# Layer norms over the partition axis: a provisional mean while the residual is made, elementwise sums of squares, a later correction of the variance

## The reference

```python
def layer_norm(x, g, b):                 # layers 0 and 1, after each residual
    mu = x.mean(-1, keepdims=True)
    var = jnp.square(x - mu).mean(-1, keepdims=True)
    return (x - mu) * lax.rsqrt(var + LN_EPS) * g + b
def rms_norm(x, g):                      # layers 2 and 3, ahead of mixer and FFN
    return x * lax.rsqrt(jnp.mean(x * x, axis=-1, keepdims=True) + EPS) * g
h = layer_norm(DN_ALPHA * h + g1 * mixer(u), ln1_g[l], ln1_b[l])
u = h * (1.0 + sc2) + sh2                # what the FFN reads
h = layer_norm(DN_ALPHA * h + g2 * swiglu(u), ln2_g[l], ln2_b[l])
```

## Time and profile before

| | us |
|---|---|
| median of 3 runs | 4056.42 (4052.18 to 4057.0) |
| the profiled execution, its own time | 4060.49 |
| its span on the engines | 4058.7 |
| PE busy | 3738.0 (92%) |
| DVE, ACT, POOL busy | 1667.6, 1322.4, 1464.4 |
| mean granted TensorE clock | 0.951 of full speed |

### The profile page before, as it was taken

The page is one execution under the profiler, slowest core; times in us unless marked ns, Lnnn a source line. Parts: engine busy times, 40 slices in busy tenths (PEclk is TensorE's granted clock), DMA queues, the critical chain, the costliest instruction groups (busy, mean ns, idle before and its releaser), DMA issues. The chain is left out here.

```text
span 4058.7 us, 38874 instructions
## 1 busy us (share of the span) xinstructions
PE 3738.0 (92%) x15948; PEld 2878.6 (71%) x15948; DVE 1667.6 (41%) x2218; ACT 1322.4 (33%) x2140; POOL 1464.4 (36%) x779
## 2 busy tenths in 40 slices
PE   4999888898999999988899899989898999899999
PEld 3887655676888688755577688857467887577887
DVE  5223554436343322455443634344545212374220
ACT  2334234322322234423432232225432222333221
POOL 1232232343455322222234345434124544204543
PEclk9998898999999999989899999999899999899999
DMA  5233211244554323421124355433015333202332
GB/s 176 83 104 104 57 42 35 72 133 120 160 167 134 114 78 94 117 55 42 37 70 132 109 169 168 135 89 90 16 37 148 96 96 91 60 13 87 94 95 77
DMA packets 566895, 385.25 MB, mean 95 GB/s; under 512 B 13518, under 2 KB 504222, under 8 KB 566718
## 3 DMA queue, kind: packets, MB, share of 16 engines
q1 hardware_dynamic: 564494, 379.56, 32.1%
q10 hardware_dynamic: 2224, 3.21, 0.3%
HBM read 379.25 MB, written 2.10 MB: 94 GB/s over the span
## 5 line engine op out<-in xcount | busy, mean ns | idle before, releaser
L144 POOL TENSOR_TENSOR wlo<-raw,whi 128x1024 fp32r<-128x1024 f32 (+2 forms) x538 | 1280.7, 2390 | 2068.2 <-ACT whi L140 2067.8
L174 PE MATMUL ps<-UH,whi 128*128 128x512 f32 x2656 | 1069.7, 403 | 57.8 <-ACT UH L140 36.8
L174 PE MATMUL ps<-UH,wlo 128*128 128x512 f32 x2656 | 1050.4, 395 | 11.3 <-POOL wlo L144 11.2
L174 PE MATMUL ps<-UL,whi 128*128 128x512 f32 x2656 | 1050.2, 395 | 5.1 <-DVE UL L144 3.9
L140 ACT ACTIVATE whi<-raw 128x1024 fp32r<-128x1024 f32 (+2 forms) x538 | 545.8, 1025 | 545.7 <-PE ps L174 253.5
L174 PEld LDWEIGHTS ps<-UH,whi 128*128 128x128 f32 x2656 | 507.6, 191 | 185.2 <-ACT UH L140 43.0
L174 PEld LDWEIGHTS ps<-UH,wlo 128*128 128x128 f32 x2656 | 507.9, 191 | 126.6 <-POOL wlo L144 18.0
L174 PEld LDWEIGHTS ps<-UL,whi 128*128 128x128 f32 x2656 | 506.6, 191 | 123.7 <-DVE UL L144 12.9
L152 DVE SCALAR_TENSOR_TENSOR ACC<-raw,SM,ACC 128x512 f32<-128x512 f32 x336 | 379.6, 1130 | 25.0 <-DMA raw<-in_w_ada 2.8
L174 PE MATMUL ps<-GH,whi 128*128 128x512 f32 x704 | 274.8, 390 | 0.0
L174 PE MATMUL ps<-GL,whi 128*128 128x512 f32 x704 | 274.0, 389 | 0.0
(11 more groups left out here) (295 smaller groups left out, 4442.9 us busy)
## 6 DMA issues: line engine op xcount, KB each, us to landing
raw<-in_w_in SPq DMA_DIRECT2D x170, 512.0 KB, 3.9
raw<-in_w SPq DMA_DIRECT2D x120, 512.0 KB, 5.2
raw<-in_w_ada SPq DMA_DIRECT2D x96, 512.0 KB, 4.9
raw<-in_ada_w SPq DMA_DIRECT2D x96, 512.0 KB, 4.5
raw<-in_ffn_w_gate SPq DMA_DIRECT2D x44, 512.0 KB, 3.9
raw<-in_ffn_w_up SPq DMA_DIRECT2D x44, 512.0 KB, 3.8
raw<-in_ffn_w_down SPq DMA_DIRECT2D x32, 512.0 KB, 3.8
raw<-in_ev_w_in SPq DMA_DIRECT2D x20, 512.0 KB, 4.0
```

Source lines behind the costliest of these rows:

```text
L144: return self.e.tensor_tensor(o, a, b, op).then_inc(*self.done(*keys))
L174: m = self.e.matmul(o, l, r, start=start, stop=stop)
```

## The change

In the layer norms:

- After residual tile 4 PE sums `CSUM` (tiles 0 to 3) into a provisional mean. DVE subtracts it (`less`) from tiles 5, 6, 7 ahead of their residual step and from 0 to 4 behind it, one instruction a tile.
- ACT squares the tiles as they come (`SQ_AT`, `SQ_ORDER`), POOL adds the squares into `P2`.
- Behind the last tile PE does four matmuls with ones: of `CSUM` (now tiles 4, 5, 6) and `H` 7 for the rest of the mean, of `P2` and the last square for the sum of squares. ACT copies the rest of the mean to `MU` and squares it, DVE corrects the variance, and DVE (tiles 0 to 3) and POOL (4 to 7) subtract `MU`.
- Scale columns `SG` and `KG` are worked out ahead. The scaled `H` for the next residual is made later (`dve_scaled`, in the first two steps of the FFN or at the start of attention).

In all norms from n1 on: `nrm` is one instruction `H*SG*R`; ACT adds the shift as it makes `UH`, and DVE as it makes `UL`. POOL's tiles are now 3, 5, 7, with a second DVE instruction for the shift. The RMS columns are made ahead of the last residual tile.

```diff
     def lo_lane(nid, kt):
-        return "pool" if nid != "n0" and kt in (1, 3, 5) else "dve"
+        return "pool" if nid != "n0" and kt in (3, 5, 7) else "dve"
+    def dve_u(v, nid, shift, centred):
+        sq, _, _, R, _ = norm_tiles(nid)
+        for kt in range(NT + 1):
+            if kt < NT:
+                s = sq[kt % 2][:, :]
+                if kt > 1:
+                    v.wait_ge(*on("act", "uh", nid, kt - 2))
+                    v.wait_ge(*on(lo_lane(nid, kt - 2), "ul", nid, kt - 2))
...
+                v.stt(s, H[:, kt, :], SG[:, kt:kt + 1], R[:, :], ALU.mult, ALU.mult, None if pool else ("s", nid, kt))
+                if pool:
+                    v.wait_ge(*v.prior())
+                    v.ts(s, s, shift[:, kt:kt + 1], None, ALU.add, None, ("s", nid, kt))
+            if kt and lo_lane(nid, kt - 1) == "dve":
...
+                v.stt(UL[:, kt - 1, :], sq[(kt - 1) % 2][:, :], shift[:, kt - 1:kt], UH[:, kt - 1, :].bitcast(F32),
+                      ALU.add, ALU.subtract, ("ul", nid, kt - 1))
+    SQ_ORDER = (0, 1, 5, 2, 3, 6, 4, 7)
+    SQ_AT = {5: (0, 1, 2), 6: (3, 4, 5), 7: (6, 7)}
+    def pe_norm_ln(p, nid, rid, mod):
...
+        p.wait_ge(*on("dve", "cs", nid))
+        p.mm(od[:, :], ones, CSUM[:, :], True, False)
+        p.wait_ge(*on("pool", "p2", nid, 6))
+        p.mm(ov[:, :], ones, P2[:, :], True, False)
+        p.wait_ge(*on("dve", "H", rid, 7))
+        p.mm(od[:, :], ones, H[:, 7, :], False, True, ("dsum", nid))
+        p.wait_ge(*on("act", "sq", nid, 7))
+        p.mm(ov[:, :], ones, sq_tile(nid, 7)[:, :], False, True, ("var", nid))
+    def dve_norm_ln(v, nid, rid, g, b, mod):
...
+        v.wait_ge(*on("act", "dc", nid))
+        centre(0)
+        centre(1)
...
+        v.stt(R[:, :], ps(("var", nid))[:, :], 1.0 / D, P2[:, :], ALU.mult, ALU.subtract, ("var", nid))
+        centre(2)
+        centre(3)
+        v.wait_ge(*on("act", "sd", nid))
+        v.recip(R[:, :], R[:, :])
+    def pool_norm_ln(g, nid):
+        MU = norm_tiles(nid)[4]
+        g.wait_ge(*on("act", "dc", nid))
+        for kt in range(4, NT):
+            g.wait_ge(*on("act", "sq", nid, SQ_ORDER.index(kt)))
+            g.tt(H[:, kt, :], H[:, kt, :], MU[:, :], ALU.subtract, ("Hd", nid, kt))
     def dve_residual(...):
+                elif m == 4:
+                    v.wait_ge(*on("pe", "prov", nid))
+                    for x in (5, 6, 7):
+                        v.wait_ge(*kept(x))
+                        less(x, ("pre", nid, x))
...
+                    less(0, ("Hp", nid, 0))
+                    less(1, ("Hp", nid, 1))
     def act_residual(a, rid, nid, sums, chunks_to):
...
             act_split(a, chunks_to(m))
+                for j in SQ_AT.get(m, ()):
+                    a.wait_ge(*less_mean(nid, rid, SQ_ORDER[j]))
+                    if j > 2:
+                        a.wait_ge(*on("pool", "p2", nid, j - 2))
+                    a.af(sq_tile(nid, j)[:, :], H[:, SQ_ORDER[j], :], ACT.Square, ("sq", nid, j))
+    def pool_residual(g, rid, nid, sums):
+        for m in range(NT):
+            pool_split(g, soon(rid, m))
+            for j in SQ_AT.get(m, ()) if sums == "means" else ():
+                if 0 < j < 7:
+                    g.wait_ge(*on("act", "sq", nid, j))
...
+                    g.tt(norm_tiles(nid)[1][:, :], norm_tiles(nid)[1][:, :], sq_tile(nid, j)[:, :], ALU.add, ("p2", nid, j))
     def dve_ffn(v, f, nid=None):
             dve_fill(v)
+            if nid and m < 2:
+                for kt in range(4 * m, 4 * m + 4):
+                    dve_scaled(v, nid, kt)
```

More of the change, by code:

```diff
@@ L593, in dve_decay @@
         v.ts(C8, C8, 8.0, None, ALU.mult, None, "c8")
+    tiles = {}
     def norm_tiles(nid):
[L598 to L602, removed]
+        if nid not in tiles:
+            tiles[nid] = (ring("nrm", 88, 2, 512), at("nsq", 94, [128, S], F32, BASE), at("nsum", 96, [128, S], F32, BASE),
+                          at("nrd", 92, [128, S]), at("nmu", 98, [128, S], F32, BASE))
+        return tiles[nid]
@@ L616, in pool_lo @@
     def pool_lo(g, nid):
         sq = norm_tiles(nid)[0]
[L618 to L624, removed]
-        for kt in range(NT):
-            p.wait_ge(*on("act", "sqr", nid, kt))
-            p.mm(o[:, :], ones, sq[kt % 2][:, :], kt == 0, kt == NT - 1, ("tot", nid, kt))
-        if not mod:
-            o = bank(p, AUX, ("sums", nid), ("act", ("sd", "n5")))
-            for kt in range(NT):
-                p.wait_ge(*on("act", "sqn", nid, kt))
-                p.mm(o[:, :], ones, sq[kt % 2][:, :], kt == 0, kt == NT - 1, ("ton", nid, kt))
@@ L634, in dve_norm_ln @@
[L634 to L638, removed]
-            blk, jsc, jsh = mod
-            wait_ada(v, blk, jsc, jsh)
-            v.ts(S1, ad(blk, jsc), 1.0, None, ALU.add, None)
-            v.wait_ge(*v.prior())
[L643 to L650, removed]
-        v.wait_ge(*on("act", "sd", nid))
-        v.recip(R[:, :], R[:, :])
-        v.wait_ge(*v.prior())
[L654 to L691, removed]
@@ new lines, in sq_tile @@
+    def sq_tile(nid, j):
+        sq, P2, _, _, _ = norm_tiles(nid)
+        return sq[(j - 1) % 2] if j else P2
+    def pe_norm_ln(p, nid, rid, mod):
+        sq, P2, CSUM, _, _ = norm_tiles(nid)
+        od = bank(p, AUX, ("dsum", nid), ("act", ("dc", nid)))
+        ov = bank(p, AUX, ("var", nid), ("dve", ("var", nid)))
+        p.wait_ge(*on("dve", "cs", nid))
[6 more added lines that the diff above has]
+        p.mm(ov[:, :], ones, sq_tile(nid, 7)[:, :], False, True, ("var", nid))
+        if not mod:
+            o = bank(p, AUX, ("sums", nid), ("act", ("sd", "n5")))
+            for kt in range(NT):
+                p.wait_ge(*on("act", "sqn", nid, kt))
+                p.mm(o[:, :], ones, sq[kt % 2][:, :], kt == 0, kt == NT - 1, ("ton", nid, kt))
@@ L731, in act_norm_rms, with pe_residual @@
         a.af(R[:, :], ps(b)[:, :], ACT.Sqrt, ("sd", nid), scale=1.0 / D, bias=EPS_RMS)
[L732 to L743, removed]
+        act_u(a, nid, ad(mod[0], mod[2]))
+    def pe_residual(p, rid, nid, name, lay, KT, XH, XL, xw, sums, fill=False):
         for m in range(NT):
@@ L999, in act_attention, with dve_attention @@
                 scaled(n - 2)
-    def dve_attention(v, lay):
+    def dve_attention(v, lay, scaled):
         T = att[lay]
+        if scaled:
+            for kt in range(NT):
+                scaled(kt)
         copy_v(v, lay, 0)
```

295 lines of the change are left out of this document (187 added, 108 removed).

## The result

The changed kernel takes 4062.55 us (median of 20 runs, 4053.1 to 4070.83) against 4055.32 us (20 runs beside them, 4047.48 to 4059.93): ratio 1.0014 [1.0008, 1.0021], slower by 3 to 8.5 us. The profiled execution takes 4064.89 us with a span of 4063.1.

What follows compares the result with a forecast made beforehand. PE, busy 92% of the span, was taken as the bound, with gains only in its idle time at the norms. Terms +4.0, -0.8, +2.3, -2.8 and -3.0 gave -0.3 us: 4056.1 us, no change, range 4038 to 4068.

Steps and rivals of the forecast that it cites:

- mean part: Layer norms n1 to n4: new mean and squares make the reciprocal later by 4.9, 0.2, 0.5 and 0.2 us.
- tile part: UH and UL stretch behind all norms, one DVE instruction replacing two, plus moved scaling: -6.1 us in all.
- the last add: POOL's final add of squares, behind all splits: ends at 980.9 in r0, elsewhere 2.5 us behind the last matmul.
- the turns: Centring behind the mean: DVE and POOL wait for each other, reciprocal 6.55 us behind the sum, 4.6 without.
- Its sums: PE's sums with ones behind POOL's final add, `P2` and tile 7: 1.9 us in r0.
- n2: Second layer norm: reciprocal +0.2 us, tile stretch -1.0, together -0.8 us.
- n3: Third layer norm: reciprocal +0.5 us, moved scaling delaying the filler's sum +1.8, together +2.3 us.
- n4 and n5: n4 reciprocal +0.2 us, its eight modulation-free tiles -0.5, n5's tile stretch -2.5: together -2.8 us.
- n6 to n8: RMS norms: the shorter tile stretch gives -1.25, -0.9 and -0.85 us, together -3.0 us.
- B: Rival: squares' chain on ACT and POOL decides at all four layer norms, +13.5 us, 4070; chance 0.21.
- A: Rival: POOL and DVE don't hinder each other, last add in time at layer norms, -23 us, 4033; chance 0.27.
- C: Rival: tile stretch saves nothing as next weights decide, +6 us, 4062; chance 0.52 together with the forecast.

Runs made afterwards that it cites:

- columns early: Changed kernel with the six small column instructions ahead of residual tile 1 instead of tile 7: 4061.4 us, ratio 1.0023 to the kernel before.
- scaled late: Changed kernel with the four scaled H tiles behind the second filler in the FFN's first two steps: 4061.83 us, ratio 1.0019 to the kernel before.
- the two with the old mean: Changed kernel with mean, squares and variance as before: 4045.49 us; the same with scaled H also behind the second filler: 4042.93 us.
- mean first: Changed kernel with PE completing the mean's sum ahead of the squares' sum, mean's square in the root's tile: 4051.74 us, ratio 0.9990 to before.
- PSUM centring: Changed kernel with DVE subtracting the mean for tiles 0 to 3 straight from PSUM, not ACT's SBUF copy: 4046.25 us, ratio 0.9980 to before.
- the run with the filler ahead: Changed kernel with early add, PSUM centring, scaled late, columns early, mean first, and tile 5's filler ahead of the subtractions: 4018.06 us, ratio 0.9910.

## Why the prediction was wrong

**The sum.** I had the mean part at +5.8 us (4.9, 0.2, 0.5, 0.2) and the tile part at -6.1. Measured by ratios: mean part +13, about 9 to 18, tile part -8, between -12 and -4. The step that failed is the size of the mean part: in its sum, the term for PE's two sums behind the last add was half of what they took, and the last add of n4 was put too early.

My terms were counted against the kernel before, and so must be the answer: from T4 to R the changed kernel's trace is 6.7 us longer at n1, 0.1 shorter at n2, 2.4 longer at n3 and 3.7 at n4, 12.7 together, where I had 5.8. At n1 the sum closes: forecast 4.9, the sums 1.9 longer than priced, the add 0.2 later, the turns 0.3 shorter, 6.7. At n4 too: forecast 0.2, the add 2.1 later, the sums 1.7 longer, the turns 0.3 shorter, 3.7. Counted so, the 3.0 us that the moved columns gave at n3 are already in these differences, and the tile part is some -5. That is near the -6.1 in part by luck: n1 gave nothing, and a wait behind n6 that I had not priced gave 3.6.

Against the old mean with the columns moved, the mean part is larger. T4 to R in three executions of the same mean code (changed, columns early, scaled late) against the two with the old mean gives it stage by stage: n1 +6.3, n2 +2.0 (0.85 of it the provisional sum), n3 +5.2 (3.0 of it because the columns no longer hold the old mean), n4 +1.7, together 15.

- *The last add.* The place was right: 984.66, where 980.9 on the axis of before is 984.5 here, 3.58 later. n4's add ended 4.6 us behind the last matmul, where I took 2.5.
- *Its sums.* I priced `P2` and tile 7 at 1.9 us in all. Behind a wait of 5.47 us they took 3.8, at n4 3.7. I had taken the 0.96 us a sum of the earlier trace rows, where PE came to the sums from a wait of 1.45 us, for a place where it comes from a long one. The granted clock was 0.50 at n1 and 1.00 at n2. The page "TensorE: Matmul & The Clock Gate" of the Trainium skill, Part 1, says that the throttled clock is the default and activity releases it; the rows agree: 1.04 us a matmul behind 5.47 us of waiting, 0.56 behind 1.83.
- *The order on PE.* The mean's sum stood behind the squares' wait; I took that as given, and mean first puts it at 10 us, of which 8 show at the four norms.
- *The turns.* Right: 6.55 us forecast from the sum to R, 6.25 measured from the start of ACT's copy, which follows the sum. By the PSUM centring they cost 2.6 us a norm, over my bound of 1.95: without turns I had 4.6 us, and it took 3.63.
- *n2.* -0.9 by the profiled execution, but +1.8 and +2.5 in two others of the same code. One profile is a sample where a wait depends on how splits and adds fall.
- *n3.* +3.3 by the trace, from T4 to F3, against +2.3. (From r2's step 0 it is +0.8, as the kernel before had the long way to T4.) The scaling cost 2.9 us, not 1.8; the columns ahead of the last tile, to which I gave no price, delayed T7 by 4.4 but hid behind the add.
- *r0 and r2.* The load was issued at 968.10, forecast 964.8 on before's axis, 968.4 here. That the same delay makes PE wait for `ACC` in r0 I had not carried on: 1.4 us, by the run with the filler ahead.
- *n4 and n5.* The eight sums of n4 did not get shorter: from its R to that of n5 it is 16.18 us, before 15.55, and 15.1 to 16.4 in the other traces, where I took 0.5 less. Behind n5 the mixer's first reciprocal comes 1.6 us sooner (2.5 forecast).
- *n6 to n8.* From r4 to F3, n6, 0.94 us less (1.25 forecast); n8 1.6 (0.85). n7 can't be read: behind it, to r6, the kernel before takes 222.2 us and the others 216.6 to 221.2. Not forecast: a wait of PE for the filler in the FFN behind n6 went, and with it a stretch at a lower clock. The timeline of before, then windows of before and of the changed kernel:

```profile
3103.98 1.36 PE L174 MATMUL ps<-CO,ACC 128*128 128x1 f32 x8 [1.64 <-DVE ACC L152]
```
```profile
3089.90:3117.80 27.90, 24.98 (x105) 19.94 (x104) 14.15 (x17) 6.55 (x8) 11.17 (x6) 0.94 0.46 134
```
```profile
3103.10:3127.40 24.30, 23.02 (x105) 18.84 (x104) 11.76 (x16) 6.55 (x8) 11.49 (x6) 1.00 0.54 153
```

  The same 105 matmuls take 3.6 us less: 1.64 is the wait, and 2.0 their own time (PE busy 24.98 and 23.02 us) at a mean clock of 0.94 and 1.00. And from F3 to the FFN's ninth product it is 60.3 to 60.4 us instead of 63.92 in each of the thirteen other traces.

**The signs** that I had named for the forecast came: the load at 968.10, the last add at 984.66, a centring of DVE 1.75 us long, n1 later and n2 about as before, POOL's last `UL` 15.0 us behind R ready, the wait for `ACC` behind n3. They told of the places, and not of what the sums cost there.

**The rivals.** B, the squares' chain decides everywhere, is what happened: the last add ended 6.3, 2.6, 6.8 and 4.6 us behind the last matmul at n1 to n4. Over three traces it cost 35 to 40% of B's price at n2 and n4. A, no turns and the add in time, fell for this kernel; yet with the turns, the order on PE and the add put right, the new mean gives some 25 us more than the old. C, the tile stretch saves nothing, held at n1 alone (T4 to F3 92.81 and 92.70).

## What to carry to other kernels

When a sum moves off PE, ask what then stands last and what in-order queue it shares: here the last square and one add of 1.26 us behind a split cost 13 to 17 us of the total, 11 to 16 of them at the four norms. Put first on each engine what the next engine waits for, and give an engine that shares SBUF with another an operand in PSUM. Price PE's work behind a long wait at the lower clock, and edits in series only together: the columns early gave nothing alone. Taking work off an engine can start a rival's instruction sooner, as POOL's split did in r2 when its last add went to PE.

## What the runs showed of the hardware

- A DVE instruction of 128x8 is held until POOL's split ends, as one of 128x512 is: 2.18 to 2.26 us at n1 and n3, beside 0.16 undisturbed. It need not have two inputs in SBUF, as my reading of the rows had it: the one of 2.18 us is a `TENSOR_SCALAR` with one, and in the kernel before `nrm<-H,SM` (`TENSOR_SCALAR`, 128x512) took 1.38 to 1.40 us beside POOL's `UL` and 0.55 otherwise. One with an operand in PSUM is not held, and POOL then isn't either (4.95 us for four, against 6.78). "Trainium Architecture — The Big Picture" of the Trainium skill, "What this means for kernel authors", calls the shared port pair an exclusive lock and no split of bandwidth; the rows agree, with these sizes.
- A short wait of PE can cost more than itself: behind n6 3.6 us for 1.64. In the even mixer the same code runs at 0.87 or 0.94, 7 us apart, from one trace to the next.
